# Projection units in two phases: all products of the high weights first, those of the low weights behind one wait

## What is computed

```python
def _swiglu(h, w_in, w_out):
    gu = h @ w_in
    return (jax.nn.silu(gu[..., :D_FF]) * gu[..., D_FF:]) @ w_out
...
        hn = _rms_norm(x, P['norm_mix_g'][l]) * (1.0 + sc1) + sh1
        if l % 2 == 0:
            y, h_new, lconv_new, ret_new = _even_mixer(hn, pos, P, j, st['lru_h'][j], st['lru_conv'][j], st['ret'][j])
        else:
            y, gla_new, C_new, n_new, m_new, mconv_new = _odd_mixer(
                hn, P, j, st['gla'][j], st['mlstm_C'][j], st['mlstm_n'][j], st['mlstm_m'][j], st['mlstm_conv'][j])
        x = x + g1 * y
        hn = _rms_norm(x, P['norm_ffn_g'][l]) * (1.0 + sc2) + sh2
        x = x + g2 * _swiglu(hn, P['w_ffn_in'][l], P['w_ffn_out'][l])
```

## Time and profile before

| | us |
|---|---|
| median of three runs | 1537.5 |
| lowest and highest | 1537.2 and 1539.61 |
| profiled execution, own time | 1538.78 |
| its span | 1537.2 |
| TensorE busy (share of the span) | 1428.2 (93%) |
| VectorE busy | 892.0 (58%) |
| ScalarE busy | 508.9 (33%) |
| GpSimd busy | 127.5 (8%) |
| TensorE idle, put down to weight_low | 13.2 in 9 places |

### The profile page before, as it was taken

One profiled execution on the slowest core, in us unless ns is written; L12 is line 12 of the kernel. 1 busy time (PEld: TensorE's weight loads), 2 busy tenths in 40 slices (PEclk: granted clock), 3 DMA queues, 4 the chain that ended last, 5 costly groups with the idle time before them and its releaser, 6 DMA issues.

```text
span 1537.2 us, 28543 instructions
## 1 busy us (share of the span) xinstructions
PE 1428.2 (93%) x11003; PEld 1353.7 (88%) x11003; DVE 892.0 (58%) x1613; ACT 508.9 (33%) x755; POOL 127.5 (8%) x149
## 2 busy tenths in 40 slices
PE   6899999969999999999679999987799999999997
PEld 4789898869999999999669897876699999999997
DVE  4565675578876885587764556664553433333344
ACT  4254345232222221222443334533332212222233
POOL 0000000002211220021000000000001101100100
PEclk9899999989999999999879899988899999999999
DMA  9443343325554554353222213221213223232222
GB/s 327 155 131 117 124 145 113 125 68 170 173 152 138 165 165 137 97 169 101 49 57 56 67 32 91 78 61 32 82 55 93 85 86 87 88 95 83 82 75 80
DMA packets 231853, 164.67 MB, mean 107 GB/s; under 512 B 9990, under 2 KB 218568, under 8 KB 231636
## 3 DMA queue, kind: packets, MB, share of 16 engines
q1 hardware_dynamic: 219716, 120.57, 26.8%
q0 software_dynamic: 11744, 42.75, 8.3%
q10 hardware_dynamic: 304, 0.10, 0.0%
HBM read 159.80 MB, written 3.60 MB: 106 GB/s over the span
## 4 chain that ended last, share of the span: by engine, by line
PE 75%; DVE 11%; ACT 7%; issue 4%; DMA 2%; SPq 0%; DVEq 0%; ACTq 0%; POOLq 0%
PE ring L604 67%; ACT weight_high L415 1%; DVE weight_low L420 1%; PE core_j L532 1%; DMA weight_raw<-in_c_w_in 1%; PE core_k L1317 1%; PE ring L2147 1%; PE ring L2229 1%; PE core_j L482 1%; DVE norm_rstd L614 1%; DVE norm_step L612 1%; PE core_k L1320 0%; DVE norm_step L611 0%; DVE normed_low L700 0%; DVE residual L710 0%
## 5 line engine op out<-in xcount | busy, mean ns | idle before, releaser
L604 PE MATMUL ring<-normed_high,weight_high 128*128 128x272 f32 x2128 | 454.7, 295 | 38.0 <-DVE normed_low L700 24.9
L604 PE MATMUL ring<-normed_high,weight_low 128*128 128x272 f32 x2128 | 446.2, 292 | 0.0
L604 PE MATMUL ring<-normed_low,weight_high 128*128 128x272 f32 x2128 | 445.4, 291 | 0.0
L604 PEld LDWEIGHTS ring<-normed_high,weight_high 128*128 128x128 f32 x2128 | 340.6, 192 | 49.0 <-issue 39.9
L604 PEld LDWEIGHTS ring<-normed_low,weight_high 128*128 128x128 f32 x2128 | 341.0, 192 | 0.0
L604 PEld LDWEIGHTS ring<-normed_high,weight_low 128*128 128x128 f32 x2128 | 338.9, 192 | 0.0
L420 DVE TENSOR_TENSOR weight_low<-weight_raw,weight_high 128x1024 fp32r<-128x1024 f32 x197 | 257.5, 1308 | 71.1 <-ACT weight_high L415 69.6
L415 ACT ACTIVATE weight_high<-weight_raw 128x1024 fp32r<-128x1024 f32 x197 | 206.8, 1050 | 164.7 <-PE ring L604 152.3
L604 PE MATMUL ring<-mixed_high,weight_high 128*128 128x272 f32 x960 | 203.6, 294 | 18.3 <-DVE weight_low L420 7.7
L604 PE MATMUL ring<-mixed_high,weight_low 128*128 128x272 f32 x960 | 200.7, 291 | 0.0
L604 PE MATMUL ring<-mixed_low,weight_high 128*128 128x272 f32 x960 | 199.9, 290 | 0.0
(11 more groups left out here) (403 smaller groups left out, 1166.9 us busy)
## 6 DMA issues: line engine op xcount, KB each, us to landing
weight_raw<-in_w_ffn_in SPq DMA_DIRECT2D x88, 512.0 KB, 3.7
mod_weight<-in_w_mod POOLq DMA_DIRECT2D x48, 512.0 KB, 4.2
mod_weight<-in_w_mod POOLq DMA_DIRECT2D x16, 1024.0 KB, 5.5
weight_raw<-in_w_ffn_out SPq DMA_DIRECT2D x32, 512.0 KB, 3.7
weight_raw<-in_a_w_in SPq DMA_DIRECT2D x24, 512.0 KB, 3.9
weight_raw<-in_c_w_in SPq DMA_DIRECT2D x20, 512.0 KB, 3.9
mixer_area<-in_w_mod SPq DMA_DIRECT2D x8, 1024.0 KB, 8.8
weight_raw<-in_w_ffn_out SPq DMA_DIRECT2D x16, 384.0 KB, 3.2
```

Of the source, the lines that this page charges most:

```text
L604: last = pe.matmul(PS[p.slot][:, half, 0:HALF], w[n.slot][:, k, :], x[:, k, half * HALF:(half + 1) * HALF], start=(k == 0 and w is WH and ...
```

## The change

`project` no longer calls `product` for each tile. It waits at its head for the high part and the ring. It then runs, tile by tile, the four matmuls with the high weight. Behind the last tile's it waits for the low part, and then runs the two matmuls with the low weight of every tile in a row. The waits for normed_low and for the last mixed_low tile stand in the first loop. `s_used` is counted with the last matmul, as before. The number of matmuls, their operands and sizes stay, and what each of the other engines does, too.

```diff
         def project(pe, n, p, kt=KD, moving=(HNH, HNL), normed=None, mixed=None):
-            pe.wait_ge(s_lo, n.index + 2)
+            h, l = moving
+            pe.wait_ge(s_hi, n.index + 1)
             pe.wait_ge(s_free[p.slot], p.before)
             for k in range(kt):
                 if normed is not None:
                     pe.wait_ge(s_hnl, normed + k + 1)
                 if mixed is not None and k == kt - 1:
                     pe.wait_ge(*mixed)
-                last = product(pe, n, p, k, kt, moving)
+                for x in (h, l):
+                    for half in range(2):
+                        pe.matmul(PS[p.slot][:, half, 0:HALF], WH[n.slot][:, k, :],
+                                  x[:, k, half * HALF:(half + 1) * HALF], start=(k == 0 and x is h), stop=False)
+            pe.wait_ge(s_lo, n.index + 2)
+            for k in range(kt):
+                for half in range(2):
+                    last = pe.matmul(PS[p.slot][:, half, 0:HALF], WL[n.slot][:, k, :],
+                                     h[:, k, half * HALF:(half + 1) * HALF], start=False, stop=(k == kt - 1))
             last.then_inc(s_used, 1)
```

## The result

The changed kernel takes 1530.06 us (median of 7 runs, 1524.96 to 1533.49) against 1539.61 us for the kernel before (median of 7 runs, 1537.2 to 1543.31). The ratio is 0.9947, with a 95% interval of 0.9928 to 0.9965: 5 to 11 us faster, 8 in the middle. The profiled execution takes 1528.35 us, its span is 1526.8 us, 10.4 less than before.

What follows compares the result with a forecast made beforehand. TensorE bounds the kernel; only its low-part waits, 13.2 us in nine places, could shrink. Gains of 12.5 less 3.2 and 0.2 take 9.1 off the profiled 1538.78, giving 1529.7; the median 1.3 lower gives 1528.4, range 1525.0 to 1534.5.

Steps and rivals of the forecast that it cites:

- Layer 0's last part: Layer 0's last FFN part, second unit: high part ready before its predecessor ends, so an earlier start gains 1.6 us.
- Its output projection: Layer 0's output projection, third unit: 0.60 us idle goes, with the restart a gain of 0.7 us.
- Layer 1's third unit: Layer 1's FFN, third unit: starts 1.33 us earlier and loses its half-clock stretch, 1.5 us more.
- Its last part: Layer 1's last FFN part: three pairs of output units run at TensorE's own pace, gaining 2.3 us.
- Layer 1's output projection: Layer 1's output projection, third unit: starts when its high part is done, gaining 1.33 us; its low clock stays.
- Layer 0's third unit: Layer 0's FFN, third unit: starts 2.26 us earlier and also loses its half-clock stretch.
- The clock: Third units of both FFNs: about 1.0 us idle avoids half clock, gaining 3.0 us; rival, it falls anyway, chance 0.17.
- The small unit: Layer 1's small unit: 20 matmuls instead of six remain after the last normed tile, partly at half clock, costing 3.2 us.
- The mixed tile's wait: First output unit of each FFN part: wait comes earlier, 0.5 and 0.95 us idle in last parts, 0.2 elsewhere.
- The wait in the middle of each unit: One more wait between high and low products in each of 187 units that go through project: costs nothing.
- the rival: Each mid-unit wait has a fixed price, 187 times; 0.1 us each gives 1547, sign turns at 0.05; chance 0.09.
- VectorE: Backlog after layer 0's third unit clears in two or three pairs; rival, it costs 4 us, 1532.4, chance 0.13.

Runs made afterwards that it cites:

- the order alone: Changed kernel's matmul order, but with the wait for the low part back at each unit's head and none in the middle; one run, 1544.6 us.
- the repeat: The changed kernel measured again, unedited, on the chip of the last runs, against the kernel before; median 1532.34 us of 10 runs, ratio 0.9955.
- the halves outside: Against the order alone: in the high products the column halves loop outside, high and low activation inside; one run, 1545.78 us.

## Why the prediction was right, and where it was off

- The forecast was 1528.4, range 1525.0 to 1534.5, with 9.1 us gained; measured are 1530.06 and 8 us by the ratio. The forecast started from a median of 1537.5 (three runs); that of seven is 1539.61. The places by themselves gave less than 9.1, about 6 us (below), so the closeness of the two gains is in part luck; the interval of 5 to 11 us holds both.
- **The late starts.** Layer 0's last part: predicted 1.6, measured 1.64. Its output projection: predicted 0.7, measured 0.6. Layer 1's third unit: predicted 1.33 + 1.5, measured 2.76. Its last part: predicted 2.3, measured 2.33; here the measured starts and not the idle values gave the right size. Layer 1's output projection gave 0.8 instead of 1.33: the low clock lay over 4.3 us of the unit instead of 3.3. Layer 0's third unit was to give 3.76 us; it gave 3.53, and the 1.35 ahead of it were a gift of the clock.
- **The clock.** Right for both units. In all ten places in five traces where a third unit began after 0.91 or 0.99 us of idle time and ran in the new order, it ran at full clock. Where it began after 3.17 or 2.25 us (four traces, both layers), half clock followed each time, as it did after 2.06 us at the fourth unit. But the premise that 1.98 us does no harm was luck: the same stop was followed by half clock in one trace of three. Near 2 us the length of one idle time doesn't tell what the clock will do.
- **The small unit.** Right in mechanism and place, and the clock did stay low until the block of 20. The term was 3.2, measured 2.7, since the clock rose some 2.2 us into the block and not 3.2. That 3.2 was no good reading to begin with: the low stretches of the two FFN units ended 4.4 and 4.8 us into them. It was 3.05 with the order alone, 3.04 in the repeat, and 3.89 with the halves outside, where the low clock lay over the whole block: within the bounds of 1.75 and 4.2.
- **The mixed tile's wait.** Right in place, a little smaller than reckoned: 0.27 and 0.77 us of idle time at the two last parts for 0.5 and 0.95, and no such wait in the four parts with 8 tiles.
- **The wait in the middle of each unit.** Zero was right for the wait. But the step "nothing", for 187 units, failed for what came with it: I had priced the new order of the matmuls at nothing without a sentence on it. It costs 0.02 to 0.03 us a unit, 2.6 us over the 108 units of the long stretches. Elsewhere the changed kernel's shifts show 0.4 us more (0.15 and 0.14 in the output projections, 0.1 in layer 0's mixer), so about 3.0 us in all; the 4.3 in the expectation of the repeat, at one rate for all 187 units, was too much. The rate is half of the 0.05 us at which the rival turns the sign. Measured by the shifts, the places gave 0.56 + 3.53 + 1.64 + 0.79 + 2.76 + 2.33 = 11.6 us, where 12.5 were forecast; less 2.7 and 3.0 that is 5.9 us, under the 8 measured in the middle. The difference is within the interval and of the size of the clock's play.
- **VectorE.** The backlog was worked off in three pairs as reckoned: the shifts of the low parts of the third unit and of the fifth to the eighth are -0.84, -1.79, -2.59, -3.58, -4.37. What I had missed is that the fourth unit, too, needed the new order.

## What to carry over

A wait for an operand belongs ahead of the first instruction that reads it, and before the order of work is changed for its sake, move the wait alone: here it gave as much as reordering every unit, without its costs. Then reorder only the units whose operand is really late, and count the unit behind each of them as well, for its own operand may have been hidden by the first one's delay. Deferring work to the end of a unit costs wherever that unit is fed piece by piece and its result is on the path.

## What the hardware showed that I had not expected

- The same 48 matmuls take 6.01 us in one order and about 0.013 or 0.033 us more in another, with the same operands, full clock and no idle time.
- A satisfied wait with its register step in a busy stream of matmuls costs nothing that 54 units can show: 339.51 against 339.52 us in the old order, 341.05 both ways in the new.
- The same stop of 1.98 us, ahead of the same unit, left the clock at 2.4 GHz in two traces and brought it to 1.2 in a third. Two stops with four matmuls between them are no sure remedy either: after 0.99 and 0.42 us it stayed at 2.4, after 0.91 and 1.49 us it fell.
